# Router logits taken from the un-normalized residual, and the gather of expert tokens split in two

## What is computed

```python
h2 = rmsnorm(x, norm2_w) * (1 + mod[4]) + mod[3]
aff = softmax(h2 @ w_router, axis=-1)              # 256 tokens x 16 experts
gate, idx = lax.top_k(swapaxes(aff, 1, 2), 32)     # each expert takes its 32 best tokens
xe = h2[bidx, idx]
a, u = einsum(xe, w_gate), einsum(xe, w_up)        # 16 experts, 1024 x 1408 each
ye = einsum(silu(a) * u, w_down) * gate
x = x + mod[5] * scatter_add(ye at idx)
out = rmsnorm(x, final_norm_w)
```

## Time and profile before

| | us |
|---|---|
| median of 3 runs | 1383.29 (1382.21 to 1385.93) |
| span of the profiled execution | 1385.5 |
| PE busy | 1013.7 (73%) |
| DVE, ACT busy | 529.2 (38%), 289.4 (21%) |
| moved | 415.13 MB, mean 300 GB/s |

### The profile page before, as it was taken

One profiled execution on the slowest core, in us unless ns is written; L12 is line 12 of the kernel. 1 busy time (PEld: TensorE's weight loads), 2 busy tenths in 40 slices (PEclk: granted clock), 3 DMA queues, 4 the chain that ended last, 5 costly groups with the idle time before them and its releaser, 6 DMA issues.

```text
span 1385.5 us, 12873 instructions
## 1 busy us (share of the span) xinstructions
PE 1013.7 (73%) x5366; PEld 582.6 (42%) x5366; DVE 529.2 (38%) x983; ACT 289.4 (21%) x457; POOL 28.7 (2%) x42
## 2 busy tenths in 40 slices
PE   1797888799899997989887755555565656566574
PEld 0675767676576786677664211111111111011121
DVE  6976666775651697576754100000000000000002
ACT  3422343552331444542411000000000000000000
POOL 0000000100000001000010000000000000000000
PEclk9997889999999998899986978888867786767787
DMA  9895211577534576232376999999999999999994
GB/s 389 324 379 223 92 61 62 222 272 274 213 119 155 183 288 255 91 122 92 122 290 263 424 430 431 431 431 428 431 430 430 431 430 430 431 431 431 431 430 182
DMA packets 41001, 415.13 MB, mean 300 GB/s; under 512 B 4912, under 2 KB 4912, under 8 KB 7792
## 3 DMA queue, kind: packets, MB, share of 16 engines
q1 hardware_dynamic: 38160, 405.75, 71.8%
q10 hardware_dynamic: 2784, 8.57, 1.7%
HBM read 413.26 MB, written 1.05 MB: 299 GB/s over the span
## 4 chain that ended last, share of the span: by engine, by line
PE 41%; DMA 40%; DVE 13%; ACT 4%; issue 1%; POOL 1%; DVEq 0%; POOLq 0%; ACTq 0%
DMA ring<-in_w_egu 24%; DMA ring<-in_w_ed 12%; PE PS L633 7%; PE PS L634 7%; PE PS L635 7%; PE PS L934 3%; PE PS L1238 3%; DMA arena<-in_w_ed 2%; DVE ringR L1438 2%; PE PS L555 2%; PE PS L1300 2%; DMA ring<-in_w_in 1%; DVE arena L1315 1%; ACT ringR L2332 1%; PE PS L1288 1%
## 5 line engine op out<-in xcount | busy, mean ns | idle before, releaser
L1238 PE MATMUL PS<-ring,arena 128*32 128x512 f32 (+1 forms) x1152 | 174.8, 742 | 110.8 <-DMA ring<-in_w_egu 110.8
L633 PE MATMUL PS<-ringR,arenaR 128*128 128x512 f32 (+1 forms) x520 | 217.2, 418 | 31.6 <-DVE arenaR L1426 24.1
L634 PE MATMUL PS<-ringR,arenaR 128*128 128x512 f32 (+1 forms) x520 | 209.6, 403 | 0.0
L635 PE MATMUL PS<-ringR,arenaR 128*128 128x512 f32 (+1 forms) x520 | 209.1, 402 | 0.0
L1438 DVE TENSOR_TENSOR ringR<-ring,ringR 128x2048 fp32r<-128x2048 f32 (+1 forms) x66 | 148.7, 2254 | 105.5 <-ACT ringR L2332 100.5
L1315 DVE SCALAR_TENSOR_TENSOR arena<-arena,PS 128x256 f32<-128x256 f32 (+2 forms) x68 | 33.2, 498 | 373.9 <-ACT arena L2749 366.8
L2332 ACT ACTIVATE ringR<-ring 128x2048 fp32r<-128x2048 f32 (+1 forms) x66 | 123.9, 1884 | 88.0 <-PE PS L635 61.6
L1238 PEld LDWEIGHTS PS<-ring,arena 128*32 128x32 f32 x1152 | 36.5, 129 | 238.2 <-DMA ring<-in_w_egu 172.9
L1300 PE MATMUL PS<-ring,arena 128*32 128x512 f32 x512 | 86.4, 809 | 57.1 <-DMA ring<-in_w_ed 56.5
L633 PEld LDWEIGHTS PS<-ringR,arenaR 128*128 128x128 f32 x520 | 100.6, 194 | 59.0 <-DVE arenaR L1426 31.0
L555 PE MATMUL PS<-CT,arena 128*128 128x128 f32 (+1 forms) x352 | 65.3, 335 | 79.2 <-DVE arena L1315 27.6
(11 more groups left out here) (328 smaller groups left out, 865.5 us busy)
## 6 DMA issues: line engine op xcount, KB each, us to landing
ring<-in_w_egu SPq DMA_DIRECT2D x48, 2048.0 KB, 35.8
ring<-in_w_ed SPq DMA_DIRECT2D x32, 2048.0 KB, 34.6
ring<-in_w_vad SPq DMA_DIRECT2D x40, 1024.0 KB, 7.0
ring<-in_w_egu SPq DMA_DIRECT2D x24, 1536.0 KB, 30.0
arena<-in_w_egu SPq DMA_DIRECT2D x16, 2048.0 KB, 35.3
arena<-in_w_ed SPq DMA_DIRECT2D x12, 2048.0 KB, 32.6
ring<-in_w_in SPq DMA_DIRECT2D x22, 1024.0 KB, 4.8
ring<-in_w_gu SPq DMA_DIRECT2D x22, 1024.0 KB, 4.8
```

What stands on the lines that cost most here:

```text
L633: mm(o, xh(k, t), hi[:, c], start=k == 0, stop=False)
L634: mm(o, xh(k, t), s.viewr[:, c], start=False, stop=False)
L635: i = mm(o, xl(k, t), hi[:, c], start=False, stop=k == nk - 1)
L1238: i = mm(PS[32 * ee:32 * ee + 32, b + a_, 0:fw], XEv[:, k, grp, 32 * ee:32 * ee + 32], wv[:, ee, a_, :], start=k == 0, stop=k == 7, tile_p ...
```

## The change

1. The transposes take X itself, group g of 512 columns and tile t as soon as `v out2 x` of that quarter is there; the evictions are plain copies into `XT` (ACT for g = 0, DVE for g = 1). The router's weights are multiplied by the norm's per-channel factor ahead of time (`RT`, in the lane `decays`), the shift's share of the logits is computed once by eight matmuls in the lane `gla` (`pe rt bias`, copied to `BT`), and the root is applied to the 128 x 16 logits by one DVE operation for each t.
2. The scaled tokens and their high half are made by ACT (`normed`), not by DVE.
3. The selection matrix and the gather are split: first the 4 experts of group 0 (128 columns), later the other 12 (384 columns), after the eight `gate_up(0, 0, k)`. PE now does `gathered_first(0)`, `(1)`, then `gate_up(0, 0, 0)`.

The diff, cut to its core; the first piece is PE in the lane `gla` behind `pe gla in` 3, then PE behind `out2`, PE's expert steps, DVE in `decays` (second step), DVE in `gla`, DVE's softmax:

```diff
+                w.wait_ge(*at("v nr affine"))
+                for k in range(8):
+                    i = mm(PS[:, 0, 0:16], affs2[:, 24 + k:25 + k].broadcast_to([128, 128]), PR("router", 16 * k, 16 * k + 16), start=k == 0, stop=k == 7)
+                i.then_inc(*sig("pe rt bias"))
...
-            norm_turned("nr", junkf, (0, 1, 2, 3), lambda k, t: [at("a gate row", 3)], lambda k: logits(k - 2) if k else None)
-            logits(6)
+            for g, t, b in ((0, 0, 2), (0, 1, 3), (1, 0, 6), (1, 1, 7)):
+                w.wait_ge(*at("v out2 x", g, t))
+                w.wait_ge(*at("a gate row", 3))
+                for j in range(4):
+                    i = tr(PS[:, b, 128 * j:128 * j + 128], Xv[:, t, 512 * g + 128 * j:512 * g + 128 * j + 128])
+                i.then_inc(*sig("pe nr tr", g, t))
+            w.wait_ge(*at("v rt w"))
+            for t in range(2):
+                for g in range(2):
+                    w.wait_ge(*at("v nr xt" if g else "a nr xt", t))
+                    for k in range(4 * g, 4 * g + 4):
+                        i = mm(PS[:, 4 * t, 0:16], XT[:, 1024 * t + 128 * k:1024 * t + 128 * k + 128], RT[:, 16 * k:16 * k + 16], start=k == 0, stop=k == 7)
+                i.then_inc(*sig("pe rt lg", t))
...
-            for k in range(10):
+            for k in range(9):
                 if k < 8:
-                    gathered(k)
-                if k > 1:
-                    w.wait_ge(*at("a rt xe" if k % 2 == 0 else "v rt xe", k - 2))
-                    gate_up(0, 0, k - 2, 0)
+                    gathered_first(k)
+                if k > 0:
+                    w.wait_ge(*at("a rt xe" if k % 2 else "v rt xe", k - 1))
+                    gate_up(0, 0, k - 1, 0)
+            for k in range(8):
+                gathered_rest(k)
...
+                affine("nr", mc2, 16, 0, PR("n2"), affs2[:, 16:32])
+                chain()
+                tt(RT.rearrange("p (k n) -> p k n", k=8), PR("router").rearrange("p (k n) -> p k n", k=8), affs2[:, 16:24].unsqueeze(2).broadcast_to([128, 8, 16]),
+                   ALU.mult).then_inc(*sig("v rt w"))
...
+                w.wait_ge(*at("pe rt bias"))
+                cp(BT, PS[:, 0, 0:16]).then_inc(*sig("v rt bias"))
...
-            high2(0)
             for t in range(2):
+                w.wait_ge(*at("g nr rs", t))
                 w.wait_ge(*at("pe rt lg", t))
-                e.tensor_reduce(s4[:, t:t + 1], PS[:, 4 + t, 0:16], AX.X, ALU.max).then_inc(*sig("v rt"))
+                stt(AFv[:, t, :], PS[:, 4 * t, 0:16], st4[:, 4 + t:5 + t], BT, ALU.mult, ALU.add).then_inc(*sig("v rt"))
+                chain()
+                e.tensor_reduce(s4[:, t:t + 1], AFv[:, t, :], AX.X, ALU.max).then_inc(*sig("v rt"))
```

More of the change, by code:

```diff
@@ L2159, in vector @@
             next(lanes["r"])
-            affine("nr", mc2, 16, 0, PR("n2"), affs2[:, 16:32])
             low("out2", 3)
@@ L2228, in vector @@
             for k in range(1, 8, 2):
[L2229 to L2230 removed]
+                w.wait_ge(*at("pe rt xe2", k))
+                ts(XEv[:, k, 1:4, :], PS[:, 4 + k % 4, 0:384].rearrange("p (g s) -> p g s", g=3), affs2[:, 16 + k:17 + k], affs2[:, 24 + k:25 + k],
+                   ALU.mult, ALU.add).then_inc(*sig("v rt xe2", k))
             w.wait_ge(*at("pe rt sgt", 0))
@@ L2718, in scalar, with squared, normed @@
             gate_row(3, 2, mods2[:, 1024:2048])
[L2719 to L2728 removed]
+            def squared(g, t):
+                c = slice(512 * g, 512 * g + 512)
+                w.wait_ge(*at("v out2 x", g, t))
+                act(two(junkf)[:, t, c], Xv[:, t, c], ACT.Square, scale=1.0 / 32, accum_out=st4[:, 2 * g + t:2 * g + t + 1]).then_inc(*sig("a nr sq", g, t))
+            def normed(t):
+                c = slice(1024 * t, 1024 * t + 1024)
+                w.wait_ge(*at("g nr rs", t))
+                chain()
+                act(junkf[:, c], Xv[:, t, :], ACT.Identity, scale=st4[:, 4 + t:5 + t]).then_inc(*sig("a nr xn", t))
+                chain()
+                act(H2[0][:, c], junkf[:, c], ACT.Copy).then_inc(*sig("a rt h1", t))
+            for g, t in ((0, 0), (0, 1), (1, 0)):
+                squared(g, t)
+            for t in range(2):
+                w.wait_ge(*at("pe nr tr", 0, t))
+                act(XT[:, 1024 * t:1024 * t + 512], PS[:, 2 + t, :], ACT.Copy).then_inc(*sig("a nr xt", t))
+            squared(1, 1)
+            normed(0)
             for t in range(2):
                 w.wait_ge(*at("v rt mx", t))
[L2731 removed]
+                act(AFv[:, t, :], AFv[:, t, :], ACT.Exp, bias=s4[:, t:t + 1], accum_out=s4[:, 2 + t:3 + t]).then_inc(*sig("a rt ex", t))
+            normed(1)
             w.wait_ge(*at("v nr affine"))
@@ L2734, in scalar @@
                 w.wait_ge(*at("pe rt xe", k))
-                act(XEv[:, k], PS[:, 4 + k % 4, :].rearrange("p (g s) -> p g s", g=4), ACT.Identity, scale=affs2[:, 16 + k:17 + k], bias=affs2[:, 24 + k:25 + k]).then_inc(*sig("a rt xe", k))
+                act(XEv[:, k, 0, :], PS[:, 4 + k % 4, 0:128], ACT.Identity, scale=affs2[:, 16 + k:17 + k], bias=affs2[:, 24 + k:25 + k]).then_inc(*sig("a rt xe", k))
+            for k in range(0, 8, 2):
+                w.wait_ge(*at("pe rt xe2", k))
+                act(XEv[:, k, 1:4, :], PS[:, 4 + k % 4, 0:384].rearrange("p (g s) -> p g s", g=3), ACT.Identity,
+                    scale=affs2[:, 16 + k:17 + k], bias=affs2[:, 24 + k:25 + k]).then_inc(*sig("a rt xe2", k))
             w.wait_ge(*at("pe rt sgt", 1))
```

73 lines of the change are left out of this document (29 added, 44 removed).

## The result

| | before | after |
|---|---|---|
| median, 17 runs each | 1385.95 us (1382.21 to 1394.33) | 1375.93 us (1372.76 to 1384.31) |
| ratio after / before | | 0.993, 95% interval 0.9918 to 0.9942 |
| span of the profiled execution | 1385.5 us | 1374.3 us |

The change makes the kernel 0.7% faster, some 10 us. Two later sets of runs, in which it stood beside the kernel before again, gave 0.9898 [0.9866, 0.9931] and 0.9903 [0.9888, 0.9918], 12.8 and 13.5 us. The forecast was 6.0 us, so the direction was right and the size too small; the rest of this document is about the missing 5 us.

A forecast was written before the change was run, and what follows sets the result against it. The expert-weight stream bounds the kernel, its end following the stream's start and the first expert step's end. 7.8 us gained less 1.8 in the mixer gives 6.0, from 1383.29 to 1377.3 us; range 1373.0 to 1380.8.

The forecast's parts named there:

- The bound: Expert-weight stream from 762 us to the end: the kernel's end follows the stream's start and the first expert step's end.
- T1: End of the first expert step, `gate_up(0, 0, 0)`, which the ninth transfer needs: 747.1 for 754.93, before the mixer's 1.8 us loss.
- the break of 4.7 us: Pause left in the weight transfers ahead of the ninth, where 12.5 us stood before.
- mixer: Eight bias matmuls on PE ahead of `pe ret ot`: 1.8 us lost, passed on in full; bounds 0 to 2.2.
- from `out2` to the affinities: Transposes, logits and softmax behind `out2`: 6.0 us gained (4.8 to 7.9), affinities ending about 731.9.
- gathers and first step: Two narrow gathers at 0.457 us a matmul, 3.66 us, then `gate_up(0, 0, 0)`, ending at 747.1.
- The logits: the rival: Clock holds through the logits as PE is no longer idle behind `out2`: logits end 728.2, time 1375.4; chance 0.15.
- the same fall at 726.1: PE's clock falls during the logits, 3.8 us after `out2`, as before; logits end at 730.1.
- The rival with 0.225: Narrow gather is cheap, 0.225 us a matmul: first expert step ends 745.9, time 1376.0; chance 0.22.
- The clock's rise: PE's clock rises 6.1 us after the gathers began, at 746.5, within the first gate-and-up step.
- A second break: Another stop of the transfers, near 790 us; would prove the forecast wrong, which had 8.8 us of cover.
- The slower rival: First third of the expert steps stays at the low clock: 12.7 us slower, 1396.0; chance 0.05.

The follow-up runs named there:

- e1: Kernel before plus only the eight bias matmuls on PE, the affine ahead of time and the copy of the bias: 1387.01 us, ratio 0.9995.
- e5: Changed kernel with the eight bias matmuls and their copy moved ahead to about 615 us, where PE waits: 1373.72 us, ratio 0.9896.
- e6: Changed kernel with the bias matmuls moved to about 615 us and three filler matmuls in PE's wait ahead of `ret ot`: 1370.5 us, ratio 0.9905.
- e4: Kernel before plus three matmuls whose result nobody reads, on PE between `out2` and the transposes: 1384.52 us, ratio 0.9989.
- e8: Changed kernel with ring places 4 and 6 released to expert weights after their own last users in the mixer: 1372.83 us, ratio 0.989.
- e9: Changed kernel with bias matmuls at about 615 us, fillers ahead of `ret ot` and around the top 32, places 4 and 6 released early: 1372.16 us, 0.9902.
- e2: Kernel before with only the split of selection and gather (part 3 of the change): 1382.22 us, ratio 0.9974.
- e7: Changed kernel with filler matmuls on PE while DVE finds the top 32, and between the steps behind it: 1373.08 us, ratio 0.9902.

## Why the prediction came out as it did

**The bound was right.** The end follows T1: 11.3 us earlier (754.93 to 743.64), landing 11.1 us earlier, 12.5 us of span on the common scale with the tail's 1.4. The profiled spans differ by 11.2 because the changed kernel's offset was +1.28. The forecast of T1, 7.8 earlier less 1.8, was too small by 5.3 us, and the break of 4.7 us that it left is nearly gone with them. Term by term, forecast and measured:

| step | forecast | measured | where |
|---|---|---|---|
| mixer | -1.8 | -0.1 | `out2` ends 722.10, then 722.18 |
| from `out2` to the affinities | +6.0 | +8.1 | end 737.86, then 731.13 - 1.28 = 729.85 |
| selection | +0.85 | +0.8 | affinities to gathers 9.41, then 8.62 |
| gathers and first step | +1.0 | +2.5 | 7.66, then 744.92 - 739.75 = 5.17 |
| T1 | +6.0 | +11.3 | |

- *The mixer: the step that failed in its mechanism.* "Passed on in full, since after 672.67 ACT, DVE and POOL follow each other up to 701.28" is true up to 701.28 and was taken to hold beyond. The matmuls ran for 1.86 us as priced (at 680, not 671), and `ret ot` was 1.6 us later. What the text didn't ask is at which clock PE works around that point. Some 20 us of matmuls follow it, and before, the first of them ran at the low clock, with PE idle for 2.14 us ahead of `ret ot`. In the changed kernel the pause was 1.24 us, and the clock stayed up, which gave the 1.6 us back. The bias matmuls don't fill the pause. It is shorter because the product ahead of it, started 1.6 us later, ran at the low clock for longer and lost 0.9 us, which nobody waited for. e1 shows this with nothing else changed, and e5 in reverse; e6 fills the pause itself, and the clock stays up as well. That delay and gain cancel to 0.1 us is luck as far as these runs tell. What sets the time of the rise in that product, 695.4 or 698.8, stays open.
- *The logits: the rival had the size.* "I take the same fall at 726.1" took the fall as tied to the time behind `out2`. The clock held to 730.8, 7 us behind `out2`'s end, and the logits ended at 725.86 + 3.64 - 1.28 = 728.2, to the tenth the bound for a clock that holds, which had 0.15. Against it the text had put that transposes ran before, too; but before, PE had waited 2.17 us ahead of them, and now it waited 0.20. e4 shows that filling such a pause moves the fall by 3.4 us. The rival's reason, that PE is no longer idle behind `out2`, is still not shown as the cause: in e6 PE is idle there as little, and the clock falls inside the logits, at 725.8, nearly the time of the forecast. The Trainium skill, "TensorE: Matmul & The Clock Gate", section "Part 4: PE-mode transpose", says that a transpose doesn't count as PE being busy in the same way. These runs don't decide on it: 16 transposes and 32 narrow matmuls behind `out2` ran at 1.00 to their end in the changed kernel, and not in e6.
- *The gather: a term mis-sized.* 0.457 us a matmul was taken from the top bound, on the ground that a float32 matmul of 16 columns takes 0.42. From start to start it is 0.24 at the low clock for 128 columns, and at the high one (745.44 - 744.85) / 4, some 0.15. The rival with 0.225 was right, and had 0.22. The float32 row was the wrong neighbour, because it is two instructions: per instruction it is 0.21 us, and 0.24 is near that. By the Trainium skill, same page, sections "LDWEIGHTS" and "Back-to-back issue gap", four take an estimated 0.43 us; the trace has 0.95, so the rule gives less than half of it, and the forecast's 1.83 is nearly double. An estimate of load and matmul one behind the other by that page of the Trainium skill, 0.21 us, is the nearest of the three.
- *The clock's rise* came 4.7 us behind the first gather, not 6.1. With the gathers over so soon it matters little: the first step took 3.28 us, at the low clock nearly throughout.
- *Selection*, *`normed`, evictions, affinities beside other work*: as forecast. ACT's exponential for t = 1 waited 1.39 us for DVE, not for `normed`.
- *A second break* didn't come; `gate_up(0, 1, 0)` starts at 771.24, and every 4 us from 760 to 816 move 389 GB/s or more. The slower rival needed the first third at the low clock; it was high from 744.4 through the last of its steps.

The two likeliest rivals, clock held and cheap gather, came together. The text has 1373.2 us for that, with a gather cheap by proportion; with the 0.225 us of the rival, close to the 0.24 measured, its sum gives 1377.3 - 1.9 - 1.3 = 1374.1. (By the same sum "by proportion 1375.3" should be 1375.1.) That the range held the median of the runs, 1375.93, is in part luck: the kernel before had 1385.95 beside it. Against the forecast's own yardstick of 1383.29 the measured ratio 0.993 gives 1373.6, the two later sets under 1370, and the last landing of the traces, 11.1 us earlier, 1372.2, which is just below the range. The mixer's term, the logits' clock and the gather's price all erred to the same side.

## What to carry to other kernels

- Follow a delay past the point where its chain joins the next stage, and look at the granted clock of the stretches ahead of that point and behind it. Here a delay of 1.6 us changed where PE ran at the low clock, 0.9 us lost where nobody waited and 1.6 us gained where somebody did. Adding the delay in full was wrong, and so would be the rule that a delay is always given back.
- Don't take the time at which the clock fell in the old trace as given, nor the pauses in front of PE as the whole answer. In e4 a filled pause moved the fall by 3.4 us; in e6 the clock fell 5.0 us behind `out2`'s end, in the changed kernel 6.9, with PE waiting no longer in e6. Carry both cases as rivals with their prices.
- A stream behind a ring has two starts, the first transfer and the first release. Measure how far apart they are: once a change has brought them together, an earlier start gives little by itself (0.6 us of landing for 16 us of start in e8). Both together, in e9, gave 1.9 us of landing.
- Set traces on one scale by a row ahead of the change before subtracting. Here the offset was as large as the effects, and without it e6's gain would have read as 3 us.

## What the runs showed of the hardware

- Narrow float32r matmuls, from start to start: 128 columns 0.24 us each at 1.2 GHz (1.90 / 8, e2) and about 0.15 at 2.4 GHz; 512 columns 0.45 at 1.2 GHz, (752.69 - 747.27) / 12, and 0.28 at 2.4 GHz, (755.99 - 754.86) / 4, both before the change; 384 columns 5.92 / 32 = 0.185 at 2.4 GHz with the tail. A quarter of the columns is half of the time.
- Pauses of 2.1 to 2.2 us at `ret ot` came with a fall of the clock (before, e2, e4, e5); pauses of 0.2 to 1.3 us at the same place with none (the other ten executions).
- Sixteen transposes and 32 instructions of 16 columns behind dense work ran at 2.4 GHz in the changed kernel. The same sequence in e6 and e9 lost the clock inside the logits, 5.0 us behind `out2`'s end, though PE waited only 0.2 us. What decides between the two stays open.
- e7: filler in PE's wait raised the clock from 733.5 to 736.9, and it was down again from there on, though PE was busy for 1.64 of the 2 us around the fall and 1.80 of the next 2; so the gathers at 738.75 had nothing of it.
